# Waits for each input transfer, an early value tile, and score copies on two engines in a two-block transformer kernel

## The reference: what is computed

```python
def rmsnorm(x, g):
    xf = x.astype(jnp.float32)
    y = xf * lax.rsqrt(jnp.mean(xf * xf, axis=-1, keepdims=True) + RMS_EPS)
    return (y * g.astype(jnp.float32)).astype(x.dtype)
...
    proj = h @ w_in
    (fq, fk, fv, f_logit, nq, kc, vc, ksl, vsl, kwn, vwn,
     nsa_gate_logit, merge_logit) = split_columns(proj, IN_SPLITS)
...
    q = (hf @ wq).reshape(T, PEER_HEADS, 2, PEER_QDIM // 2)
    s = jnp.einsum('thpd,hpnd->thpn', q, subkeys).astype(jnp.float32)
    s1, i1 = lax.top_k(s[:, :, 0], PEER_TOPK)
    s2, i2 = lax.top_k(s[:, :, 1], PEER_TOPK)
...
        act = jax.nn.gelu(jnp.einsum('cd,chkd->chk', x_c, u[idx_c]).astype(jnp.float32), approximate=False)
```

## Time and profile before

| what | us |
|---|---|
| median of 3 runs | 1780.29 (1780.14 to 1781.65) |
| the profiled execution | 1776.18 |
| its span | 1774.4 |
| TensorE busy with products | 1666.5 (94%) |
| VectorE busy | 1192.9 (67%) |
| ScalarE busy | 894.6 (50%) |
| mean granted TensorE clock | 0.971 of full |

### The profile page before, as it was taken

One profiled execution on the slowest core, in us unless ns is written; L12 is line 12 of the kernel. 1 busy time (PEld: TensorE's weight loads), 2 busy tenths in 40 slices (PEclk: granted clock), 3 DMA queues, 4 the chain that ended last, 5 costly groups with the idle time before them and its releaser, 6 DMA issues. The chain is left out here.

```text
span 1774.4 us, 34027 instructions
## 1 busy us (share of the span) xinstructions
PE 1666.5 (94%) x13054; PEld 1470.4 (83%) x13054; DVE 1192.9 (67%) x2003; ACT 894.6 (50%) x1559; POOL 70.0 (4%) x35
## 2 busy tenths in 40 slices
PE   6979989799999999989999999996989999899988
PEld 5878778799999999988888888794767898788877
DVE  4556656579989799986666666654645657645665
ACT  4335644254554677765666665632644644233333
POOL 0000000000000000000000000000001333100000
PEclk9979999999999999999999999996999999999999
DMA  5532144455555444436666666540122444200004
GB/s 192 181 114 84 60 127 148 145 172 159 183 170 173 148 130 132 127 120 195 190 195 194 190 192 197 166 148 25 60 66 90 154 143 144 95 3 2 3 25 143
DMA packets 63077, 230.02 MB, mean 130 GB/s; under 512 B 7009, under 2 KB 7265, under 8 KB 62833
## 3 DMA queue, kind: packets, MB, share of 16 engines
q1 hardware_dynamic: 62960, 228.39, 40.7%
HBM read 227.32 MB, written 1.05 MB: 129 GB/s over the span
## 5 line engine op out<-in xcount | busy, mean ns | idle before, releaser
L1048 DVE TENSOR_TENSOR tile_low<-weights,tile_high 128x1024 fp32r<-128x1024 f32 x252 | 307.2, 1222 | 144.0 <-ACT tile_high L1038 140.2
L1038 ACT ACTIVATE tile_high<-weights 128x1024 fp32r<-128x1024 f32 x252 | 268.0, 1063 | 136.8 <-issue 136.8
L175 ACT ACTIVATE tile_high<-weights 128x1024 fp32r<-128x1024 f32 x169 | 178.0, 1057 | 258.2 <-issue 78.7
L187 DVE TENSOR_TENSOR tile_low<-weights,tile_high 128x1024 fp32r<-128x1024 f32 x146 | 180.0, 1237 | 172.0 <-ACT tile_high L175 151.6
L1100 PE MATMUL banks<-parts,tile_high 128*128 128x256 f32 x2048 | 271.4, 286 | 7.9 <-PEq L974 7.9
L1100 PEld LDWEIGHTS banks<-parts,tile_high 128*128 128x128 f32 x2048 | 255.6, 193 | 8.0 <-issue 8.0
L1402 PE MATMUL banks<-tile_high,parts 128*128 128x512 f32 x1024 | 254.8, 392 | 4.7 <-ACT parts L1367 4.7
L1402 PEld LDWEIGHTS banks<-tile_high,parts 128*128 128x128 f32 x1024 | 193.4, 189 | 45.0 <-issue 4.9
L227 PE MATMUL banks<-parts,tile_high 128*128 128x272 f32 (+1 forms) x1216 | 170.3, 293 | 4.2 <-PEq L442 3.4
L227 PEld LDWEIGHTS banks<-parts,tile_high 128*128 128x128 f32 x1216 | 157.0, 191 | 19.3 <-issue 16.8
L1105 PE MATMUL banks<-parts,tile_low 128*128 128x256 f32 x1024 | 145.4, 285 | 9.2 <-DVE tile_low L1048 9.2
(11 more groups left out here) (379 smaller groups left out, 2257.6 us busy)
## 6 DMA issues: line engine op xcount, KB each, us to landing
weights<-in_peer_u SPq DMA_DIRECT2D x128, 512.0 KB, 3.5
weights<-in_peer_v SPq DMA_DIRECT2D x128, 512.0 KB, 3.5
weights<-in_dn_in SPq DMA_DIRECT2D x49, 512.0 KB, 3.5
weights<-in_in_t SPq DMA_DIRECT2D x19, 512.0 KB, 3.5
weights<-in_attn_t SPq DMA_DIRECT2D x19, 512.0 KB, 3.5
weights<-in_in_m SPq DMA_DIRECT2D x16, 512.0 KB, 3.6
weights<-in_wq SPq DMA_DIRECT2D x16, 512.0 KB, 3.5
weights<-in_dn_out SPq DMA_DIRECT2D x16, 512.0 KB, 3.6
```

What stands on the lines that cost most here:

```text
L175: k.nc.scalar.activation(k.high[:, m % 2, :], k.ring.view(n), ACT.Copy).then_inc(*k.high_made.up())
L187: unit.tensor_tensor(k.low[:, m % 2, :], k.ring.view(n), k.high[:, m % 2, :].bitcast(F32), ALU.subtract).then_inc(*k.low_made[engine].up())
L1038: k.nc.scalar.activation(k.high[:, (s + j) % 2, :], k.ring.buf[:, j % RING, :], ACT.Copy).then_inc(k.high_made.sem, 1)
L1048: k.nc.vector.tensor_tensor(k.low[:, (s + j) % 2, :], k.ring.buf[:, j % RING, :], k.high[:, (s + j) % 2, :].bitcast(F32), ALU.subtract).th ...
```

## The change

Three parts of the first block change.

1. **Input transfers.** The input stage is gone. Its loads are issued by SyncE in the first lines of the `in_t` block (`fetch_inputs`), x as two transfers of 512 KB, each with its own semaphore, then the common constants, the first weight tile, the parameters, three more tiles, and the first stage's constants last. Each engine waits for what it reads, where it reads it. VectorE sets one column of `norms` to 1, and ScalarE takes a root of it before it squares x. SyncE waits for the first stage's constants before it goes on to the fifth tile.
2. **Value tile.** The high and low parts of the first `in_fv` tile are made at the end of the `in_t` block.
3. **Scores.** The sub-key tiles go to places 2 and 3 of the ring. Of the four score copies VectorE keeps two and ScalarE gets two. TensorE runs two products of `keep_busy` after the scores.

```diff
--- before.py
+++ after.py
@@ -109,8 +109,10 @@
     group("merge_first", d["in_m"][0:MERGE_FIRST])
     group("cmp_w1", d["cmp_w1"])
     group("merge_rest", d["in_m"][MERGE_FIRST:N_MERGE])
-    for name in ("branch", "out1", "wq", "subk"):
+    for name in ("branch", "out1", "wq"):
         group(name, d[name])
+    r.next = 2
+    group("subk", d["subk"])
     r.align()
     k.tiles["u"] = len(r.slots)
     for j in range(NKEY):
@@ -308,6 +310,7 @@
     summed, chain, rooted, scaled, turned = k.start("norm_summed", "norm_chain", "norm_rooted", "norm_scaled",
                                                     "norm_turned")
     parted, left = k.start("norm_high", "norm_low")
+    cleared, loaded = k.start("norm_cleared", "root_table_loaded")
     high, low = k.pair(cols)
     starts = [sum(rows for _, rows in tiles[:i]) for i in range(len(tiles))]
     t = len(tiles)
@@ -318,19 +321,26 @@
     ahead = range(k.tiles[following] + (1 if halves else 0), k.tiles[following] + AHEAD)
 
     def sync(sp):
+        if not halves:
+            fetch_inputs(sp, k)
         for dst, src in fetch:
             sp.dma_start(dst, src).then_inc(*k.fetched.up(16))
         load_tiles(sp, k, k.prefetch)
 
     def scalar(act):
         if not halves:
+            act.wait_ge(*cleared.at(1))
+            nc.scalar.activation(k.norms[:, 47:48], k.norms[:, 47:48], ACT.Sqrt).then_inc(*loaded.up())
             for i, (h, rows) in enumerate(tiles):
+                act.wait_ge(*k.x_landed[i].at(16))
                 nc.scalar.activation(scratch[0:rows, i, :], h, ACT.Square,
                                      accum_out=sums[0:rows, i:i + 1]).then_inc(*summed.up())
         act.wait_ge(*chain.at(3 if scaled_rows else 2 if halves else 1))
         nc.scalar.activation(root, y, ACT.Sqrt).then_inc(*rooted.up())
         for m in ahead:
             make_high(act, k, m)
+        if not halves:
+            act.wait_ge(*k.param_landed.at(16))
         for c in range(KC):
             act.wait_ge(*turned.at(c + 1))
             nc.scalar.activation(high[:, c, :], ps[:, c, 0:cols], ACT.Copy,
@@ -345,6 +355,8 @@
             done(nc.vector.tensor_scalar(step[:, 1:t], y[:, t:n], EPS, None, ALU.mult))
             done(nc.vector.scalar_tensor_tensor(y[:, 1:t], sums[:, 1:t], 1.0 / D, step[:, 1:t], ALU.mult, ALU.add))
         else:
+            if not halves:
+                nc.vector.memset(k.norms[:, 47:48], 1.0).then_inc(*cleared.up())
             if halves:
                 done(nc.vector.tensor_tensor(sums, sums, k.norms[:, 40:40 + n], ALU.add))
             else:
@@ -352,11 +364,15 @@
             done(nc.vector.tensor_scalar(y, sums, 1.0 / D, EPS, ALU.mult, ALU.add))
         dve.wait_ge(*rooted.at(1))
         newton(nc, dve, chain, y, root, inv, step)
+        if not halves:
+            dve.wait_ge(*k.common_landed.at(16))
         for i, (h, rows) in enumerate(tiles):
             nc.vector.tensor_scalar(diagonal(i), k.ident[0:rows, 0:rows], inv[0:rows, i:i + 1], None,
                                     ALU.mult).then_inc(*scaled.up())
         for m in ahead:
             make_low(dve, k, m)
+        if not halves:
+            dve.wait_ge(*k.param_landed.at(16))
         for c in range(KC):
             dve.wait_ge(*parted.at(c + 1))
             nc.vector.scalar_tensor_tensor(low[:, c, :], ps[:, c, 0:cols], weight[:, c:c + 1],
@@ -383,7 +399,7 @@
             "turned": turned}
 
 
-def project_T(k, name, chunks, n, write, prefetch, norm):
+def project_T(k, name, chunks, n, write, prefetch, norm, following=None):
 
 
 
@@ -420,6 +436,8 @@
                 if engine(i) == "vector":
                     dve.wait_ge(k.ring.used.sem, first + i + 1)
                     put(dve, i, ps[:, i % 8, 0:2 * n if n == S else n]).then_inc(*by["vector"].up())
+                if following is not None and i == chunks - 2:
+                    make_low(dve, k, k.tiles[following])
 
         @block.scalar
         def _(act):
@@ -430,6 +448,10 @@
                 if engine(i) == "scalar":
                     act.wait_ge(k.ring.used.sem, first + i + 1)
                     put(act, i, ps[:, i % 8, 0:n]).then_inc(*by["scalar"].up())
+            if following is not None:
+                make_high(act, k, k.tiles[following])
+    if following is not None:
+        k.split_early.add(k.tiles[following])
 
 
 def project_N(k, name, lhs, groups, prefetch, following):
@@ -488,19 +510,16 @@
                 make_low(dve, k, n)
 
 
-def input_stage(k):
-    nc = k.nc
-    got, = k.start("inputs_landed")
-    with nc.Block() as block:
-
-        @block.sync
-        def _(sp):
-            for dst, src in ((k.h, k.dram["x"]), (k.common[:, :], k.dram["const_common"]),
-                             (k.param[:, :], k.dram["param"]),
-                             (k.const1, k.dram["const_first"])):
-                sp.dma_start(dst, src).then_inc(*got.up(16))
-            load_tiles(sp, k, RING)
-            sp.wait_ge(*got.last())
+def fetch_inputs(sp, k):
+
+    for tt in range(NT):
+        sp.dma_start(k.h[:, tt, :], k.dram["x"][:, tt, :]).then_inc(*k.x_landed[tt].up(16))
+    sp.dma_start(k.common[:, :], k.dram["const_common"]).then_inc(*k.common_landed.up(16))
+    load_tiles(sp, k, 1)
+    sp.dma_start(k.param[:, :], k.dram["param"]).then_inc(*k.param_landed.up(16))
+    load_tiles(sp, k, RING)
+    sp.dma_start(k.const1, k.dram["const_first"]).then_inc(*k.const_landed.up(16))
+    sp.wait_ge(*k.const_landed.last())
 
 
 def prepare_stage(k):
@@ -970,7 +989,9 @@
 
     nc, ps = k.nc, k.ps
     first = k.tiles["subk"]
-    taken, = k.start("scores_taken")
+    taken, stored = k.start("scores_taken", "scores_stored")
+    place = lambda tt, q: (k.score[:, tt, 8 * q:8 * q + 8, :].rearrange("p a n -> p (a n)"),
+                           ps[:, 4 * tt + 2 * q:4 * tt + 2 * q + 2, :].rearrange("p b n -> p (b n)"))
     with nc.Block() as block:
 
         @block.sync
@@ -988,11 +1009,17 @@
                                                k.qT[:, 8 * q + a, tt * P:tt * P + P], keys[:, a, :],
                                                start=True, stop=True)
                 tile_used(ins, k, first + q)
+            pe.wait_ge(*taken.at(1))
+            keep_busy(k, 0, 2)
 
         @block.scalar
         def _(act):
             for n in early(k, "u"):
                 make_high(act, k, n)
+            for q in range(2):
+                act.wait_ge(k.ring.used.sem, first + q + 1)
+                dst, src = place(1, q)
+                nc.scalar.activation(dst, src, ACT.Copy).then_inc(*stored.up())
 
         @block.vector
         def _(dve):
@@ -1000,10 +1027,8 @@
                 make_low(dve, k, n)
             for q in range(2):
                 dve.wait_ge(k.ring.used.sem, first + q + 1)
-                for tt in range(NT):
-                    src = ps[:, 4 * tt + 2 * q:4 * tt + 2 * q + 2, :].rearrange("p b n -> p (b n)")
-                    nc.vector.tensor_copy(k.score[:, tt, 8 * q:8 * q + 8, :].rearrange("p a n -> p (a n)"),
-                                          src).then_inc(*taken.up())
+                dst, src = place(0, q)
+                nc.vector.tensor_copy(dst, src).then_inc(*taken.up())
 
 
 def top16(nc, dve, sig, values, top, index):
@@ -2813,12 +2838,14 @@
         (sum((n for _, n in k.const_cols['first'][0])),))
     k.vcmp = k.vcmp[0:N_CMP, :]
     k.bind("first", k.const1)
-    input_stage(k)
+    k.x_landed = k.start("x_landed_0", "x_landed_1")
+    k.common_landed, k.param_landed, k.const_landed = k.start("common_landed", "param_landed",
+                                                                          "const_first_landed")
     norm = norm_programs(k, [(k.h[:, tt, :], P) for tt in range(NT)], k.p("norm_mix"), S, "in_t", halves=False)
 
     project_T(k, "in_t", MERGE, S,
               (lambda i: "vector", lambda eng, i, src: sum_halves(k, k.T[:, i, :], src)),
-              k.tiles["in_fv"] + RING, norm)
+              k.tiles["in_fv"] + RING, norm, following="in_fv")
     def copy(dst, banks):
         def finish():
             for tt in range(NT):
```

## The result

The changed kernel took **1758.5 us** in the median of 4 runs (1758.0 to 1760.2), the kernel before beside it 1780.8 (1780.1 to 1781.7): a ratio of 0.988, with a 95% interval of 0.987 to 0.989. The gain is 22.3 us.

A forecast was written before the change was run, and what follows sets the result against it. TensorE, busy 94% of the span, was taken as the bound; gains come from its idle or lower-clock stretches. 6.4 + 1.1 + 6.3 + 1.5 = 15.3, and 1780.3 - 15.3 = 1765.0 us; range 1761.0 to 1769.5.

The forecast's parts named there:

- Part 1: Inputs at the start: x awaited alone, no table load before the root, first product at about 8.9; 6.4 us saved.
- The table rule: ScalarE's loads at the start: 1.28 us each by the rows; 2.66 per switch by the skill, which would give 1762.2.
- rival 5: Table loads at the start hold ScalarE longer than their row, giving 2.6 us more, 1762.4; chance 2%.
- Part 2: Value tile at the end of `in_t`: both parts hidden, TensorE starts sooner; 1.1 us saved, bounds 0 and 2.2.
- Part 3: Scores: shorter wait before the expert stage saves 6.3 us; clock staying at 2.4 GHz saves 1.5 more.
- what lies behind the three places: Later stages: both engines shift together, no fixed wait swallows the earlier start; no further gain or loss in the sum.
- Rival 3: Lower-clock stretches, such as 109 to 136 us, grow or shrink: 3.4 us either way, 1768.4 or 1761.6; chance 12%.
- The scaling step: Whole kernel: the profiled 1776.18 minus 15.3 is 1760.9; the median lies 4.1 higher, so 1765.0 against it.
- Rivals 1: Start: x lands in a crowd, its second half at 8.33; part 1 gains 3.7, time 1767.7; chance 8%.
- 2: Scores: the clock falls all the same, or VectorE's picks are the true limit; 1766.5; chance 10%.
- 4: `in_t` stage: TensorE stutters and stays at 1.2 GHz, 53 us more, 1818; chance 2%.
- 6: Start: SyncE's wait or table work stands before the squares, so part 1 gives nothing; 1771.4; chance 2%.

The follow-up runs named there:

- the control: The kernel before, unchanged, run again: 1780.9 us, ratio 1.000; its profiled execution took 1781.74 us.
- c8: Changed kernel without the root ahead of the squares (VectorE's 1 and ScalarE's root), so a second table load returns: 1759.4 us.
- c4: Kernel before with only the scores change (ring places, copies on two engines, two idle products): 1768.5 us, ratio 0.994.
- c7: Kernel before with VectorE's last score copy made twice: 1779.5 us, ratio 0.999.
- c14: Kernel before with some score products of the second tile made three times and four idle products behind the first score copy: 1778.0 us.
- c2: Kernel before with only the input change (fetch_inputs, root ahead, the waits): 1771.3 us, ratio 0.995.
- c13: Kernel before with four idle products in TensorE's wait at the 81st expert tile: 1780.2 us, ratio 1.000.
- c17: Kernel before with one low part of the second block given to VectorE instead of GpSimd: 1777.8 us, ratio 0.999.
- c5: Changed kernel without the two idle products behind the scores: 1761.2 us, ratio 0.989.
- c6: Changed kernel with the sub-key tiles in ring places 1 and 2 again: 1764.9 us, ratio 0.992.
- c15: Kernel before with the fills of c13 and c14, and one idle product on each side of `in_t` to `in_fv`: 1775.6 us.
- c1: The same run as the control, the kernel before unchanged: 1780.9 us, ratio 1.000.
- c16: Changed kernel with four idle products behind the last `in_vv` tile and four in the 81st tile's wait: 1759.7 us, ratio 0.989.

## Why the prediction was wrong

The mechanisms of the three parts held. The sum had two terms at nothing: the slowed products behind two pauses, which I let cost what they cost in one execution, and a wait in the second block that an earlier start removes. By the traces of the control and of the changed kernel, the lead grows so (differences of the moments at which the same instruction starts; they are one slow execution of the one and a quick one of the other, hence 23.8 and not 22.3):

| stretch | lead gained, us | forecast |
|---|---|---|
| start to the first `in_t` tile | 4.9 | 6.4 |
| to the first `in_fv` product | 1.2 | 1.1 |
| `in_fv`, to the first score product | 2.9 | 0 |
| scores, to the first expert product | 5.5 | 6.3 |
| the first expert tile's 16 products | 1.6 | 1.5 |
| from there to 800 us, with the wait of 2.90 | 3.1 | 0 |
| behind 800 us | 4.6 | 0 |
| sum | 23.8 | 15.3 |

In total TensorE stands still 14.0 us less (104.7 in the control, 90.7 after) and its products take 9.8 less (1675.3 and 1665.5).

- **Part 1: right, mis-sized.** I had x's first half landing before 4.3 and its square over by 5.65. It landed at 5.0, so both squares stand behind it: 9.49 instead of 8.9. Then the 32 products took 6.63 instead of the 6.27 I had left unchanged ("within 1 us either way"). Part 1 gave 5.5 against the execution before, 4.9 against the control.
- **The table rule.** By the Trainium skill (ScalarE: Activation LUTs, section What ACT_TABLE_LOAD costs) each switch would cost a drain beside the load. c8 puts one load back and its first product is 1.12 later: less than the load's 1.28. No drain is seen, the rows stand, and rival 5 is out.
- **Part 2: right**, 1.2 for 1.1. But the pause had a second price, which I excluded by the row for 8 products in 2.11. In the control, c4, c7 and c14 the 8 took 3.0 or more; in c2, c13 and c17 they took 2.11 behind the same pause.
- **Part 3: right to 0.1** for the waiting and the clock. Wrong about its pieces: in c5 the clock holds there without the idle products, and they cost 0.73 each, not 0.49, though under cover. The ring places carry most of it (6.4 in c6, 1.8 of it by the idle products).
- **The failed step is the one on what lies behind the three places**, which the sum has at 0. "A fixed wait that would swallow an earlier start I don't find" looked for losses only. Two gains stood there. The first is the lower clock behind the pauses at 77 and before the 81st tile: c15 measures 4.7 for these and the scores without any shorter wait, and 1.5 of that was in the sum. The second is the collision in the second block with what follows it: 2.4 in c17, and 2.7 to 2.9 in the traces of c17, c2, c4 and the changed kernel. Together that is some 6 of the 7.0 by which the sum was short, and part 1 was over-sized besides, so the account isn't closed to the microsecond. Rival 3 named the first mechanism, that a pause's effect on the clock depends on its moment, but priced another stretch (109 to 136 us) and held a loss as likely as a gain. The pause at 77 was shortened; that the wait before the 81st tile mostly costs nothing in the changed kernel is what the traces show, without a reason.
- **The scaling step.** I took the 4.1 us between the profiled execution and the median for an offset that the change leaves alone. Against the control's trace it was the lower clock behind the pauses, most of which the quick execution didn't have: of the 21 runs of the kernel before beside the control, one took 1776.3, the next 1778.7. Had I asked what those 4.1 us consist of, the range would have reached lower.
- **The collision** of the two low parts I didn't look for. It stood in the trace of the kernel before as a low part of 3.23 beside 1.22, with TensorE 0.89 idle behind it.

Rivals 1, 2, 4 and 6 are out: x landed before the rest, the gain at the scores is whole, the `in_t` products ran without stutter, and the squares waited for x alone.

What stays open: 1.7 us of the last row of the table, between 800 and 1360. It comes in steps of 0.8 at the first tiles behind 800 us, 0.5 between 1205 and 1218, and 0.4 behind that, and no run here tries them. In the row from `in_fv` to the scores, 1.3 of the 2.9 lie behind the first tile of `in_fv` and are open too. And which moment of a pause costs what can't be said from the rows shown here. Kernels c17 and c1 and the one before are the same up to 1472 us, and at the same wait of 2.90 they lost 1.5, 2.7 and nothing.

## What to carry to other kernels

Profile the unchanged kernel again before costing a change: two executions 5 us apart show which pauses carry a second price, and a profiled time below the median is a list of losses that the profile doesn't show. Cost a pause of 2 to 3 us in front of dense products as its own length and, as an upper bound, 1.5 to 2.7 us of slowed products behind it. A fill that shortens no wait measures that price by itself, if it is sized by the instructions that a call really makes and if the executions agree more closely than the price. And look for instructions of one form with two durations: here one of them hid 2.7 to 2.9 us.

## What the runs showed of the hardware

- Behind pauses of TensorE of 2.22 and 2.90 us the following products ran at full speed in some executions and were slowed by 1.6 and by 1.5 or 2.7 us in others, with the same instructions; behind 1.05 and 1.58 no loss was seen. Behind the pause of 3.38 in the changed kernel 16 products took 3.65, and 2.15 where c16 filled it.
- Two subtractions of 128x1024 on VectorE and GpSimd didn't run side by side: started 0.24 after GpSimd's (2.39), VectorE's took 3.23 instead of 1.22; started 0.04 before it, VectorE's took 1.21 and GpSimd's 3.43. The Trainium skill (SBUF — State Buffer, section SBUF: two separate sides) describes a pair of ports that the two share as an exclusive lock, taken by the first to start for its whole instruction; the rows agree.
- A table load of ScalarE took 1.28, with 0.01 to 0.02 to the instruction behind it, at the start and in c8 alike.
